# Keeping a layer's four query weight slabs on chip for both tiles of a two-layer decoder trunk

## The reference

```python
def chunk(xc):                                   # 128 tokens
    q = (xc @ w_query).reshape(c, PEER_HEADS, 2, half)          # 1024 x 1024
    scores = jnp.einsum('chpd,hpnd->chpn', q, sub_keys)
    s1, i1 = lax.top_k(scores[:, :, 0], 16); s2, i2 = lax.top_k(scores[:, :, 1], 16)
    ...                                          # best 16 of the 256 pairs, per head
    u = expert_u[ids]                            # 8 heads x 16 experts per token
    pre = jnp.einsum('chkd,cd->chk', u, xc)
    act = gate * jax.nn.gelu(pre, approximate=False)
    return jnp.einsum('chk,chkd->cd', act, expert_v[ids])
```

## Time and profile before

| | |
|---|---|
| three runs, median | 1595.6 us (1594.88 to 1596.59) |
| the profiled execution | 1595.76 us |
| its span, first to last instruction | 1593.9 us |
| busy: PE, DVE, POOL, ACT | 1152.5, 1066.4, 576.6, 563.6 us |
| DMA moved | 619.54 MB, of which gathers 536.90 and plain loads and stores 81.47 |

### The profile page before, as it was taken

How to read it: one execution, slowest core, us unless ns; L and a number is a source line. 1 busy time by engine, 2 the same in 40 slices (tenths; PEclk the granted TensorE clock), 3 DMA queues, 4 the chain that set the end, 5 groups by cost and what they waited for, 6 DMA issues and landing times.

```text
span 1593.9 us, 18219 instructions
## 1 busy us (share of the span) xinstructions
PE 1152.5 (72%) x6364; PEld 450.4 (28%) x6364; DVE 1066.4 (67%) x2691; ACT 563.6 (35%) x1781; POOL 576.6 (36%) x516
## 2 busy tenths in 40 slices
PE   7995577785557976786667887797666867676676
PEld 6771133350113532243112443245111311111112
DVE  3468987658996347665997636756899664444444
ACT  0503465232343236422333425623233343333331
POOL 0004434444442324333452432443444443333330
PEclk9995778996779979797677997798576886766667
DMA  9248999999999999999999999999999999999991
GB/s 369 84 166 352 421 407 403 412 418 420 421 422 389 420 419 420 421 419 418 421 421 383 412 417 420 393 392 419 420 421 421 380 423 420 423 421 420 422 421 79
DMA packets 93069, 619.54 MB, mean 389 GB/s; under 512 B 10032, under 2 KB 10544, under 8 KB 27440
## 3 DMA queue, kind: packets, MB, share of 16 engines
q0 software_dynamic: 73728, 536.90, 81.5%
q1 hardware_dynamic: 19248, 81.47, 13.0%
HBM read 617.28 MB, written 1.05 MB: 388 GB/s over the span
## 4 chain that ended last, share of the span: by engine, by line
DVE 31%; DMA 30%; PE 28%; ACT 7%; issue 3%; POOL 1%; SPq 0%; DVEq 0%; POOLq 0%; ACTq 0%
DMA ring<-in_rows,ids 30%; DVE ring L1000 14%; PE acc L482 9%; PE bank L733 4%; PE bank L633 3%; PE bank L783 3%; PE bank L516 2%; DVE wb L1278 2%; DVE part_id L1330 1%; PE bank L770 1%; PE bank L521 1%; ACT L818 1%; DVE top_i L1275 1%; DVE top_i L1285 1%; ACT diag L823 1%
## 5 line engine op out<-in xcount | busy, mean ns | idle before, releaser
L482 PE MATMUL acc<-ring,diag 64*64 64x512 f32 x4096 | 715.9, 808 | 350.4 <-ACT diag L823 347.8
L456 POOL DMA_INDIRECT ring<-in_rows,ids x512 | 576.4, 1126 | 970.8 <-PE acc L482 796.3
L1000 DVE CUSTOM_DVE_ANT_0 ring<-ring,xc 128x1024 f32<-128x1024 f32 x512 | 615.7, 1222 | 383.0 <-DMA ring<-in_rows,ids 380.7
L818 ACT ACTIVATE gel<-pre 128x1 f32<-128x1 f32 x512 | 103.4, 202 | 841.8 <-DVE pre L1000 829.5
L482 PEld LDWEIGHTS acc<-ring,diag 64*64 64x64 f32 x4096 | 145.0, 162 | 872.4 <-ACT diag L823 764.8
L823 ACT ACTIVATE diag<-cst,act_w 128x64 f32<-128x64 f32 x512 | 178.1, 348 | 16.7
L820 ACT ACTIVATE act_w<-gate,gel 128x1 f32<-128x1 f32 x512 | 150.7, 294 | 16.7
L633 PE MATMUL bank<-wring,hT 128*128 128x512 f32 x128 | 61.8, 629 | 4.5 <-DVE hT L1037 3.7
L783 PE MATMUL bank<-wring,hT 128*128 128x512 f32 x128 | 59.0, 608 | 0.7 <-DVE hT L1037 0.7
L733 PEld LDWEIGHTS bank<-hT,wring 128*128 128x128 f32 x384 | 43.6, 192 | 7.3 <-issue 7.3
L733 PE MATMUL bank<-hT,wring 128*128 128x128 f32 x384 | 45.4, 277 | 0.0
(11 more groups left out here) (236 smaller groups left out, 1012.5 us busy)
## 6 DMA issues: line engine op xcount, KB each, us to landing
wring<-in_w_out SPq DMA_DIRECT2D x16, 1024.0 KB, 12.7
wring<-in_w_in SPq DMA_DIRECT2D x16, 978.0 KB, 9.9
wring<-in_w_query SPq DMA_DIRECT2D x12, 1024.0 KB, 15.7
wring<-in_w_gate SPq DMA_DIRECT2D x12, 1024.0 KB, 15.2
ring<-in_rows,ids POOLq DMA_INDIRECT x512, 14.1
ring<-in_w_in SPq DMA_DIRECT2D x8, 978.0 KB, 15.8
wring<-in_w_latent SPq DMA_DIRECT2D x4, 768.0 KB, 9.3
held<-in_w_query SPq DMA_DIRECT2D x2, 1024.0 KB, 8.2
```

The lines of the kernel that those rows point to most:

```text
L456: pool.indirect_dma_start(out=ring[:, n % RING, :], out_offset=None, in_=rows, in_offset=bass.IndirectOffsetOnAxis(ap=ids[:, w % 2, k:k + ...
L482: last = pe.matmul(acc[rows_of(c), r, :], diag[rows_of(r), j, :], ring[rows_of(r), j, D:][:, cols_of(c)], start=False, stop=True, skip_gro ...
L818: act.activation(gel[:, j:j + 1], pre[:, j:j + 1], ACT.Gelu).then_inc(gelued, 1)
L1000: dve.tensor_tensor_reduce(out=u, in0=u, in1=xc[:, step % 2, :], scale=1.0, scalar=0.0, op0=ALU.mult, op1=ALU.add, accum_out=pre[:, j:j + ...
```

## The change

The held buffer gets four slots (`HELD`), one for each query slab of a layer. All four are loaded ahead of the keys of tile 0, and both tiles use them. So queries leave the list of ring loads. The ring has three slots. In step 2 the ple slab goes to held slot 0 and the fourth gate slab to held slot 1, ahead of gate 2, and the last step uses three gate slabs from the ring and this one. The final row gain is loaded after the loop. The scratch of the indirect DMAs' descriptors is given as 2048 bytes, where it was left at its default.

```diff
-WRING, WSLOT = 4, 2048
+WRING, WSLOT = 3, 2048
+HELD = KT // 2
+KEPT = WRING
...
 REST_LOADS = [("latent", 0)] + [("out", k) for k in range(KT // 2)] + \
-             [("query", k) for k in range(1, KT // 2)] + [("keys", 0)]
+             [("keys", 0)]
...
-            order += [(kind, k, w - 1) for kind, k in EMBED_LOADS if w < STEPS - 1 or kind == "gate"]
+            order += [(kind, k, w - 1) for kind, k in EMBED_LOADS
+                      if w < STEPS - 1 or kind == "gate" and k < KEPT]
...
-        held = sb("held", [P, WSLOT])
+        held = sb("held", [P, HELD, WSLOT])
...
-                if (kind, k, t) == ("query", 1, 0):
+                if (kind, k, t) == ("keys", 0, 0):
                     if l:
                         sp.wait_ge(ids_ready, CHUNKS * TILES * l)
-                    load(held[:].rearrange("p (a n) -> p a n", a=2), source["query"](l, 0), held_in)
+                    for i in range(HELD):
+                        load(held[:, i, :].rearrange("p (a n) -> p a n", a=2), source["query"](l, i), held_in[i])
...
                 if (kind, k, s) == ("gate", 2, STEPS - 2):
                     sp.wait_ge(query_ready, 2 * STEPS)
-                    load(held[:].rearrange("p (a n) -> p a n", a=2), source["ple"](l, 0), held_in)
-                if (kind, k, s) == ("gate", 3, STEPS - 2):
-                    sp.wait_ge(ids_ready, CHUNKS * STEPS)
-                    load(row_gain[:], final_g.partition_broadcast(P), row_gain_in)
+                    load(held[:, 0, :].rearrange("p (a n) -> p a n", a=2), source["ple"](l, 0), held_in[0])
+                    load(held[:, 1, :].rearrange("p (a n) -> p a n", a=2), source["gate"](l, KEPT), held_in[1])
...
+            sp.wait_ge(ids_ready, CHUNKS * STEPS)
+            load(row_gain[:], final_g.partition_broadcast(P), row_gain_in)
             for t in range(TILES):
...
-                    if k == 0 and t == 0:
-                        next_of(held_in, 16)
-                    w = held if k == 0 else weights()
+                    if t == 0:
+                        next_of(held_in[k], 16)
+                    w = held[:, k, :]
...
-                        if half == 0 and k == KT // 2 - 1:
+                        if k == KT // 2 - 1:
                             last.then_inc(query_half, 1)
-                    if k:
-                        release(last)
...
                 for c in range(2):
-                    if c == 0:
-                        next_of(query_half)
-                    else:
-                        wait_products(act, "query", s)
+                    next_of(query_half)
...
-    nc = bacc.Bacc("TRN2", target_bir_lowering=False, num_devices=1)
+    nc = bacc.Bacc("TRN2", target_bir_lowering=False, num_devices=1, dynamic_dma_scratch_size=2048)
```

More of the change, by code:

```diff
@@ L288, in trunk @@
         row_gain_in = sem("row_gain_in")
-        held_in = sem("held_in")
+        held_in = [sem(f"held_in{i}") for i in range(HELD)]
         lift_read = sem("lift_read")
@@ L763, in lift @@
                 if s == STEPS - 2:
-                    next_of(held_in, 16)
+                    next_of(held_in[0], 16)
                 if s == STEPS - 1:
                     pe.wait_ge(lift_read, 2)
-                w = weights() if l < DEPTH - 1 else held
+                w = weights() if l < DEPTH - 1 else held[:, 0, :]
                 for c in range(2):
@@ L791, in embed @@
                             next_of(hT_ready)
-                        w = weights()
+                        kept = l == DEPTH - 1 and k >= KEPT
+                        if kept:
+                            next_of(held_in[1], 16)
+                        w = held[:, 1, :] if kept else weights()
                         last = gate(0, k, w)
@@ L795, in embed @@
                             last.then_inc(gate_half, 1)
-                        release(gate(1, k, w))
+                        last = gate(1, k, w)
+                        if kept:
+                            last.then_inc(gate_half, 1)
+                        else:
+                            release(last)
                         turn()
@@ L802, in embed @@
                             next_of(hT_ready)
-                        last = gate(c, k, wring[:, (len(order) - KT // 2 + k) % WRING, :])
+                        w = wring[:, (len(order) - KEPT + k) % WRING, :] if k < KEPT else held[:, 1, :]
+                        last = gate(c, k, w)
                     last.then_inc(gate_half, 1)
@@ L974, in embed @@
                 for c in range(2):
-                    if c == 0 or s == STEPS - 1:
+                    if c == 0 or s >= STEPS - 2:
                         next_of(gate_half)
```

## The result

The changed kernel runs at a median of 1581.0 us (1579.42 to 1585.2, four runs) against 1595.24 (1594.46 to 1596.59): ratio 0.9914, 95% interval 0.9894 to 0.9934. In two later series, each with the kernel before on the same chip, it was 0.9918 (0.9895 to 0.9941) and 0.9930 (0.9912 to 0.9949), so 13.7, 13.1 and 11.1 us; I use 11 to 14. The forecast was 9.5 us, 1586.2. That rival, which counts all six slabs (14.9), is about as near in two of the three comparisons and outside the interval of the third (8.1 to 14.0).

What follows compares the result with a forecast made beforehand. Prediction: DMA-bound, VectorE and TensorE in turn close behind. Slabs saved 7.5 + 2.5 = 10.0 us, less 0.5 for VectorE, 9.5 us: 1586.2 us; its own range 1583 to 1590 (chance 0.60), whole range 1580 to 1594.

Steps and rivals of the forecast that it cites:

- ledger by place: Count of slabs by place in the first three windows of gathers, 2.49 us each; sum 10.0 us, forecast 9.5.
- Window 0: Gathers of tile 0, work on tile 1: three slabs fewer behind the query projection, 7.5 us saved, bounds 0 and 9.8.
- rival 2: VectorE takes over as bound where experts are chosen; only about 3.5 us saved, 1592.2 us; chance 0.17.
- Window 1: Second window of gathers (layer 1, tile 0): 23 slab issues before and after, nothing saved.
- Window 2: Third window of gathers, up to 1112 us: 22 slabs before, 21 after, 2.5 us saved, bounds 0 and 2.5.
- Window 3: Fourth window of gathers: one slab fewer ahead of an idle DMA stretch, 0 us, bounds 0 and 2.5.
- rival 1: All six removed slabs count wherever they were: 14.9 us saved, 1580.8 us; chance 0.12.
- The start: Before the first gather: one slab fewer loaded ahead where the DMA has room, worth nothing.
- The slot less: Shorter ring, slabs issued one release later in front and output projection: TensorE waits cost 0, bounds 0 and 6.2 us.
- Rival 3: Three-slot ring makes TensorE wait in the front and at the output projection: 24 us less 9.5, 1610; chance 0.08.
- The burst of four slabs: Four query slabs issued at once at the second output slab's release, 7.9 us a slab, in time; cost 0.
- The descriptor ring: Descriptor scratch of 2048 bytes for the gathers: 0 us taken, though no row shows it.

Runs made afterwards that it cites:

- l0: Changed kernel with query slabs held in layer 0 only, layer 1 reloading three a step through the ring: 1587.53 us against 1591.7 for the kernel before.
- l1: Changed kernel with query slabs held in layer 1 only, layer 0 reloading three a step through the ring: 1586.82 us against 1591.7 for the kernel before.
- w3: Kernel before with a weight ring of three slots, still 14 query loads, gate 3 of layer 1 through a second held slot: 1597.23 us against 1593.97.
- held3_w4: Changed kernel with three held slabs and four ring slots, the fourth query slab loaded every step: 1587.45 against 1593.97 us before, again 1585.79 against 1592.29.
- tail2: Changed kernel plus two needless 1 MB loads at the last turn of window: 1582.73 us, again 1581.77 beside the changed kernel's 1581.52.

## Why the prediction was right, and where it was short

**The bound.** Right. The DMA stays at 421 GB/s in the full stretches, and loads taken out of those stretches make the kernel faster: the parts of the change tried alone are the small descriptor ring (nothing), the shorter weight ring (4.6 us slower) and the held queries (l0 and l1, 8.9 and 10.0 us over w3). What is not settled to better than 2 or 3 us is the price of a slab by its place. The ledger by place gives 10.0, 2.5, 2.5, 7.5 and -5.0 us for the changed kernel, l0, l1, held3_w4 and w3, and 11.1 to 13.7, 4.3, 5.4, 5.9 to 6.4 and -4.6 were measured. It lies outside the interval for l1 (3.2 to 7.8) and for the first comparison of the changed kernel (10.5 to 16.9), inside for the others. A ledger that also counts the slab of window 3 at full price, the upper bound that the prediction gave there, has 12.5, 5.0, 5.0, 10.0 and -2.5. It fits the changed kernel, l0 and l1 better and w3 worse; held3_w4 lies outside it, and tail2, where it has 7.5 and 9.4 to 10.5 were measured, is at its edge. No run decides between the two for good.

**Window 0, 7.5 us.** Right. The four profiles with query reloads there have 356.3 us in the mean, the eight without (held3_w4, with one, left out) 348.3: 8.0. VectorE took up the earlier rows (waits 9.8 to 2.5 us) and the first turn comes at 470.7 in place of 479.9 us, so rival 2 falls, and the 0.5 us taken off for VectorE was not needed.

**Window 1, nothing.** Right: 379.2 and 381.9 without the change, 378.2 to 379.7 with it; what is left goes with the clock at the first turn (378.2 to 379.1 us where the ple matmuls took 3.70, 379.7 to 382.3 where they took 5.5 to 5.9, over all profiles).

**Window 2, 2.5 us.** This is the term that was too small. The bytes were counted right: up to the last choice queue 1 moved 21.91 MB before and 20.86 after, one slab.

```profile
q1 hardware_dynamic: 4704, 21.91, 14.5%
```

```profile
q1 hardware_dynamic: 4432, 20.86, 14.1%
```

But the window is 382.1 and 382.3 us in the two profiles of the old order and 374.8 to 377.8 in five of the new, 6.1 us less in the mean. The clock at the turn doesn't explain it: of the five, the two with slow ple matmuls there (5.8 and 5.7 us) have 375.0 and 375.3. The shorter ring isn't the cause either, since held3_w4, with a ring of four and the same 20.86 MB, has 376.0 and 375.5. A part can be the draw, since both profiles of the old order took 1595.76 us and more. Between the two first profiles the rest shows as DMA time that lay idle and no longer does. From the turn to the output projection, before and after:

```profile
862.00:1051.00 189.00, 153.85 (x882) 73.81 (x883) 108.80 (x223) 82.21 (x244) 69.28 (x59) 0.84 0.99 399
```

```profile
853.00:1038.00 185.00, 146.59 (x881) 71.84 (x881) 108.61 (x223) 81.98 (x241) 67.66 (x59) 0.89 1.00 408
```

That is (1 - 399/421) x 189 = 9.9 us idle before and (1 - 408/421) x 185 = 5.7 after. I took the idle time as fixed. It lies where TensorE is the bound (the turn and the attention), and there TensorE is busy 153.85 against 146.59 us with the same work, at a granted clock of 0.84 against 0.89. How much of this comes with the change, and how much is the draw of the clock in one profile, is not settled: l0 and w3, which both load 24.00 MB there, have 388.6 and 382.4 us, so profiles of one load order can lie 6 us apart.

**Window 3, nothing.** Supported, but not to the last us: 324.9 before against 324.6, 325.4 and 321.9; two further slabs put there cost 0.3 us in the timed medians, though the windows of those two profiles are 2 to 3 us longer. The rate behind the last turn fell below 316 GB/s, as was to be expected with a load less:

```profile
1239.00:1254.00 15.00, 14.93 (x70) 5.18 (x68) 11.11 (x27) 5.91 (x21) 9.61 (x7) 1.00 0.82 300
```

That the total came near the 14.9 of rival 1 is, by the ledger by place, in part chance: four slabs (10.0 us) lay in full stretches, and what window 2 gave beyond its slab, for a reason that is not settled, makes up for the rest.

**The start, nothing.** Right in its reason, since the DMA has 55 and 193 GB/s in slices 2 and 3. The 2.6 us between the first two profiles came back in the next two (123.1, 123.8), so they were a draw.

**The slot less.** The waits were forecast at 0 with bounds of 0 and 6.2, and are 2.4 us, in the output projections as named. In the time w3 alone is 4.6 us slower, about what the two loads that it moves into a bound stretch should cost (5.0); the link is argued. The prediction counted these loads by windows but named no price for the ring. Rival 3 had the sign of it but not the mechanism.

**The burst of four slabs.** Right: no wait of TensorE for a held slab. The four land a median of 24.0 us after issue, in steps of some 7 us (forecast 7.9).

**The descriptor ring, nothing.** Right: ratio 1.0001 (0.9986 to 1.0016).

**What stays open.** Whether w3's 4.6 us are its two moved loads, what in window 2 beyond the one slab is the change's own, why l1 brings 5.4 us where the ledger has 2.5, what a slab at the last turn costs (anything from nothing to 2.49 us), and what spreads the runs of one kernel over 8 us.

## What to carry to other kernels

When the DMA engines are the bound, price a removed or moved transfer by its place: full price (size over rate) where a stretch is at the top rate, less at turns where a compute engine sets the pace, and nothing where the DMA stands half idle, as in the start here; count issues between the same two points of the program, since a ring of another depth moves every load behind it. An order of waits in the issuing queue does the same: a load inserted behind a wait holds all loads after it, and taking it away moved gate 3 into the full stretch unnoticed. A buffer slot given up can cost by the loads that it moves into the full stretches, even where it causes hardly any waits. And time such a change against its control on the same chip, with more than one profile of each: here one kernel's runs spread over 8 us.

## What the runs showed of the hardware

The clock that TensorE is granted after the short pause at a turn of window differs between executions of one kernel: at the first turn of the changed kernel eight matmuls of 128x512 take 5.87 us in one execution (granted clock 0.62 over the 9 us around them) and 3.70 in two others (1.00), with values such as 4.4 in other kernels at the same place. TensorE starts on the first gate slab 8.8 to 12.6 us after the first copy of the accumulator. Window 1 is up to 3 us longer with the slow clock; window 2 of the changed kernel and tail2 is not, and the times of whole executions don't follow it.

The DMA engines held 421 GB/s into SBUF over 103 us of gathers with 8 KB rows, and 418 in 351 to 372 with weight loads on a second queue beside the gathers. A descriptor scratch of 2048 bytes in place of the default did not change the rate or the time (ratio 1.0001). Beside the gathers, four slabs of 1 MB issued together landed after 13.8 to 34.0 us, one every 7 us or so.
